# Fetching the first rounds' token rows of a mixture of experts from DRAM by index, instead of gathering them with one-hot products

## The reference

```python
hn = rmsnorm(h, norm_ffn_g[l])
# top-1 group of 4, then top-2 experts of its 8; combine holds the two weights of each token
for e in range(N_EXPERTS):
    h = jax.nn.silu(xf @ w_gate[e]) * (xf @ w_up[e])
    y = y + combine[:, e:e + 1] * (h @ w_down[e])
```

## Time and profile before

| | |
|---|---|
| median of 3 runs | 910.32 us (909.59 to 910.58) |
| the profiled execution | 909.68 us |
| its span, first to last instruction | 907.9 us |
| TensorE busy | 856.5 us, 94% |
| VectorE, ScalarE, GpSimd busy | 47%, 24%, 0% |
| moved by DMA | 246.86 MB, mean 272 GB/s |
| mean granted clock of TensorE | 0.98 |

### The profile page before, as it was taken

One profiled execution on the slowest core, in us unless ns is written; L12 is line 12 of the kernel. 1 busy time (PEld: TensorE's weight loads), 2 busy tenths in 40 slices (PEclk: granted clock), 3 DMA queues, 4 the chain that ended last, 5 costly groups with the idle time before them and its releaser, 6 DMA issues.

```text
span 907.9 us, 11349 instructions
## 1 busy us (share of the span) xinstructions
PE 856.5 (94%) x4631; PEld 553.3 (61%) x4631; DVE 426.2 (47%) x811; ACT 216.2 (24%) x397; POOL 3.7 (0%) x17
## 2 busy tenths in 40 slices
PE   8999999999999999999999985999996799999986
PEld 7888888777777888888734442453641353644532
DVE  5538325677674344436787122434332214435123
ACT  6422222464444222223211110100110001100114
POOL 0000000000000100000000000000000000000000
PEclk9999999999999999999999997999997899999998
DMA  8554212122222743692589999999999999999994
GB/s 291 143 98 115 97 47 93 47 93 69 72 93 66 222 115 93 266 403 75 204 320 428 417 427 427 427 427 427 429 426 430 428 427 427 427 430 426 426 412 188
DMA packets 68839, 246.86 MB, mean 272 GB/s; under 512 B 22536, under 2 KB 46128, under 8 KB 55216
## 3 DMA queue, kind: packets, MB, share of 16 engines
q1 hardware_dynamic: 68704, 246.07, 69.3%
q10 hardware_dynamic: 80, 0.02, 0.0%
HBM read 243.98 MB, written 2.10 MB: 271 GB/s over the span
## 4 chain that ended last, share of the span: by engine, by line
PE 83%; DMA 9%; DVE 4%; issue 2%; ACT 2%; SPq 0%; DVEq 0%; ACTq 0%
PE bank L904 18%; PE bank L591 9%; PE bank L593 9%; PE bank L592 9%; PE bank L961 8%; DMA R<-w_down 5%; DMA R<-w_up 3%; PE bank L618 2%; PE bank L619 2%; PE bank L620 2%; PE bank L870 2%; PE by_side L870 2%; PE bank L989 2%; PE bank L948 2%; PE bank L990 1%
## 5 line engine op out<-in xcount | busy, mean ns | idle before, releaser
L904 PE MATMUL bank<-R,packT 128*64 128x512 f32 (+1 forms) x1004 | 187.7, 611 | 20.1 <-DMA R<-w_up 10.6
L904 PEld LDWEIGHTS bank<-R,packT 128*64 128x64 f32 (+1 forms) x1004 | 58.7, 129 | 131.1 <-issue 130.6
L1438 DVE TENSOR_TENSOR wlo<-raw,whi 128x2048 fp32r<-128x2048 f32 x33 | 75.5, 2287 | 84.8 <-ACT whi L1139 84.7
L591 PE MATMUL bank<-xnT_hi,whi 128*128 128x512 f32 x288 | 113.6, 395 | 1.8 <-DVE wlo L1438 1.8
L593 PE MATMUL bank<-xnT_hi,wlo 128*128 128x512 f32 x288 | 112.2, 389 | 0.0
L592 PE MATMUL bank<-xnT_lo,whi 128*128 128x512 f32 x288 | 112.1, 389 | 0.0
L961 PE MATMUL bank<-R,actT 128*64 128x512 f32 (+1 forms) x384 | 73.8, 628 | 7.5 <-DMA R<-w_down 7.2
L1139 ACT ACTIVATE whi<-raw 128x2048 fp32r<-128x2048 f32 x33 | 63.0, 1908 | 67.7 <-PE by_side L593 33.8
L1920 DVE SCALAR_TENSOR_TENSOR y_lo<-bank,small,y_hi 128x512 fp32r<-128x512 f32 x26 | 19.4, 751 | 91.1 <-ACT y_hi L1338 91.1
L591 PEld LDWEIGHTS bank<-xnT_hi,whi 128*128 128x128 f32 x288 | 54.1, 188 | 13.3 <-issue 2.5
L593 PEld LDWEIGHTS bank<-xnT_hi,wlo 128*128 128x128 f32 x288 | 54.1, 188 | 11.5
(11 more groups left out here) (388 smaller groups left out, 1305.9 us busy)
## 6 DMA issues: line engine op xcount, KB each, us to landing
R<-w_up SPq DMA_DIRECT2D x28, 2048.0 KB, 18.4
R<-w_gate SPq DMA_DIRECT2D x26, 2048.0 KB, 19.7
R<-w_down SPq DMA_DIRECT2D x23, 2048.0 KB, 19.6
raw<-w_in SPq DMA_DIRECT2D x17, 1024.0 KB, 5.1
R<-w_down SPq DMA_DIRECT2D x10, 1024.0 KB, 10.0
R<-w_gate SPq DMA_DIRECT2D x8, 1024.0 KB, 9.9
R<-w_up SPq DMA_DIRECT2D x7, 1024.0 KB, 11.1
raw<-w_in SPq DMA_DIRECT2D x20, 256.0 KB, 4.5
```

The lines of the kernel that those rows point to most:

```text
L591: pe.matmul(dst, hi_w, hi_x, start=start, stop=False)
L904: mm = pe.matmul(dst[s * w:(s + 1) * w, :], packT[:, c, odd * P + s * w:odd * P + (s + 1) * w], part_of(s, c) if part_of else R[2 * slots[ ...
L1438: dve.tensor_tensor(wlo[c % 2][:, :], raw[c % 2][:, :], whi[c % 2][:, :].bitcast(F32), ALU.subtract).then_inc(lo_split, 1)
```

## The change

The normed rows are made whole in float32 (`hn`) and stored to a buffer in DRAM, `hn_rows`, one row per token behind a row of zeros for places that no token fills. For rounds 0, 1 and 2 TensorE no longer multiplies rows with masks. It multiplies the mask with the tokens' numbers (`number_rows`), which gives for each of the round's 128 rows the number of its token; VectorE writes it as an integer to `row_token`, and GpSimd issues an indirect DMA that fetches the 128 rows of 4 KB from DRAM into `rows` (`fetch_rows`). TensorE turns them (`turn_fetched`), ScalarE and VectorE copy them to `packT`. There is one buffer `rows`, so a fetch waits until the one before is turned. Masks are made 128 columns at a time (`mask_rows`), all first compares ahead of all second ones, instead of tile by tile.

`hn_hi` and `hn_lo` are made in round 2 (`high_h`, `low_h`), where round 3's rows are gathered with products as before, now behind the down products. `packT` is laid out by round first, and rounds 0 to 2 all use its first half. SyncE no longer waits for `hn_lo` ahead of L445; it waits for each tile of `hn` to store it, ahead of the wait for `logits_done`.

```diff
+    hn = at("hn", [P, TT, KT, P], F32, 96)
+    rows = at("rows", [P, KT * P], F32, 132)
+    hn_rows = nc.dram_tensor("hn_rows", [SEQ + 1, D], F32, kind="Internal").ap()
...
+            for t in range(TT):
+                sp.wait_ge(hn_ready, t + 1)
+                sp.dma_start(hn_rows[1 + t * P:1 + (t + 1) * P, :], hn[:, t, :, :].rearrange("p c q -> p (c q)")).then_inc(hn_stored, 16)
             sp.wait_ge(logits_done, TT)
             sp.dma_start(R[6][:, :], flat(w_gate, 2)).then_inc(slot_loaded[3], 16)
-            sp.wait_ge(hn_lo_ready, TT)
             sp.dma_start(first_down[1][:, :], flat(w_down, 0)[:, 4 * DE:8 * DE]).then_inc(spare_loaded, 16)
...
+            def fetch_rows(r):
+                if r:
+                    pool.wait_ge(left_turned, r)
+                    pool.wait_ge(right_turned, r)
+                pool.wait_ge(row_token_ready, r + 1)
+                pool.indirect_dma_start(out=rows[:, :], out_offset=None, in_=hn_rows[:, :],
+                                        in_offset=bass.IndirectOffsetOnAxis(ap=row_token[:, r:r + 1], axis=0)
+                                        ).then_inc(rows_landed, 16)
+            pool.wait_ge(hn_stored, 16 * (TT + 1))
+            for r in range(3):
+                fetch_rows(r)
...
+            def number_rows(r, b):
+                pe.wait_ge(masks_ready, TT * (r + 1))
+                for t in range(TT):
+                    mm = pe.matmul(bank[b][:, 0:1], onehot[:, t, r % 2 * P:(r % 2 + 1) * P].bitcast(F32), token_number[:, t:t + 1],
+                                   start=(t == 0), stop=(t == TT - 1))
+                mm.then_inc(tokens_summed, 1)
+            def turn_fetched(r, n, b):
+                pe.wait_ge(rows_landed, 16 * (r + 1))
+                for c in range(4 * n, 4 * n + 4):
+                    mm = pe.transpose(bank[b][:, c % 4 * P:(c % 4 + 1) * P], rows[:, c * P:(c + 1) * P], ident[:, :])
+                mm.then_inc((left_turned, right_turned)[n], 1)
...
-            keep_warm(1)
-            gather_first()
+            number_rows(0, 0)
+            keep_warm(2)
+            number_rows(1, 1)
+            keep_warm(2)
+            for n in range(2):
+                turn_fetched(0, n, 2 + n)
...
+                if i == 1:
+                    number_rows(2, 2)
...
+                elif i == 0:
+                    for n in range(2):
+                        turn_fetched(1, n, 2 + n)
...
+                if i == 1:
+                    pe.wait_ge(main.h_added, 2)
+                    turn_fetched(2, 0, 3)
+                    pe.wait_ge(main.actT_ready, 2)
+                    turn_fetched(2, 1, 4)
+                project_down(main, slots_of(i, 2), i, 8 * (i - 1) + 3 if i else None, None if i > 1 else down_half_done)
                 if i == 2:
                     pe.wait_ge(main.h_added, 8 * i)
+                    pe.wait_ge(main.onehot_ready, 1)
+                    pe.wait_ge(hn_lo_ready, TT)
                     for n in range(2):
-                        gather_half(1, n)
+                        gather_half(n)
                     for n in range(2):
-                        turn_gathered(1, n)
-                project_down(main, slots_of(i, 2), i, 8 * (i - 1) + 3 if i else None, None if i > 1 else down_half_done)
-                if i == 1:
-                    pe.wait_ge(main.h_added, 8 * i)
-                    pe.wait_ge(main.onehot_ready, 1)
-                    for n in range(2):
-                        gather_half(0, n)
-                    for n in range(2):
-                        turn_gathered(0, n)
+                        turn_gathered(n)
...
-                act.activation(hn_hi[:, t, :, :], hg[:, t, :, :], ACT.Copy, scale=rstd[:, t:t + 1]).then_inc(hn_hi_ready, 1)
+                act.activation(hn[:, t, :, :], hg[:, t, :, :], ACT.Copy, scale=rstd[:, t:t + 1]).then_inc(hn_ready, 1)
+            def high_h(t):
+                act.activation(hn_hi[:, t, :, :], hn[:, t, :, :], ACT.Copy).then_inc(hn_hi_ready, 1)
...
+            def mask_rows(r, numbers):
+                cols = slice(r % 2 * P, (r % 2 + 1) * P)
+                for t in range(TT):
+                    dve.tensor_scalar(onehot[:, t, cols], numbers[:, cols], row_first[:, t:t + 1], None,
+                                      ALU.is_equal).then_inc(mask_step, 1)
+                for t in range(TT):
+                    dve.wait_ge(mask_step, TT * r + t + 1)
+                    dve.scalar_tensor_tensor(out=onehot[:, t, cols], in0=numbers[:, cols], scalar=row_second[:, t:t + 1],
+                                             in1=onehot[:, t, cols].bitcast(F32), op0=ALU.is_equal,
+                                             op1=ALU.add).then_inc(masks_ready, 1)
...
+            pick_rows(ranks)
+            mask_rows(0, spaced_iota)
+            number_rows(0, 0)
+            mask_rows(1, spaced_iota)
+            number_rows(1, 1)
```

More of the change, by code:

```diff
@@ L331, in build_block, with packs_done @@
         PACK_BANKS = (2, 3, 7, 4)
+        def packs_done(line, g):
+            return 4 * g - 6 if line is main else 4 * g
         SPREAD_BANKS = ((2, 3, 5, 6), (7, 0, 1, 2))
@@ L883, in gather_half, with turn_gathered, project @@
                 mm.then_inc(main.pack_done, 1)
-            def turn_gathered(r, n):
-                pe.wait_ge((rows_left, rows_right)[n], r + 1)
+            def turn_gathered(n):
+                pe.wait_ge((rows_left, rows_right)[n], 1)
                 for c in range(4 * n, 4 * n + 4):
-                    mm = pe.transpose(bank[2 + n][:, c % 4 * P:(c % 4 + 1) * P], packT[:, c, r * P:(r + 1) * P], ident[:, :])
+                    mm = pe.transpose(bank[2 + n][:, c % 4 * P:(c % 4 + 1) * P], rows[:, c * P:(c + 1) * P], ident[:, :])
                 mm.then_inc((left_turned, right_turned)[n], 1)
-            def project(line, slots, odd, dst, done, packed=None, half_done=None, part_of=None, gathered=None):
+            def project(line, slots, side, dst, done, packed=None, half_done=None, part_of=None, gathered=None):
                 for slot, loaded in slots:
@@ L1011, in fill @@
                 pe.matmul(bank[b][:, 0:n], ident[:, :], h_tok[:, 0, 0:n], start=True, stop=True)
-            keep_warm(1)
-            gather_first()
+            number_rows(0, 0)
[4 more added lines that the diff above has]
+                turn_fetched(0, n, 2 + n)
             for i in range(LAST):
                 odd = i % 2
+                side = odd if i > 2 else 0
                 if i == OVER_AT:
@@ L1304, in copy_pack, with copy_rows @@
                                    ACT.Copy).then_inc(line.pack_a, 1)
[L1306 to L1312, removed]
+            def copy_rows(n):
+                act.wait_ge(main.pack_done, n + 1)
+                act.activation(rows[:, n * 512:(n + 1) * 512], bank[2 + n][:, :], ACT.Copy).then_inc((rows_left, rows_right)[n], 1)
@@ L1319, in expert_pair @@
                 act.wait_ge(line.gate_done, i + 1)
                 act.activation(silu_g[:, :], bank[0][:, :], ACT.Silu).then_inc(line.silu_ready, 1)
[L1321 to L1324, removed]
-                    for n in range(2):
-                        copy_turned(1, n)
-                    scale_rows(line, i, odd)
-                    return
+            def expert_pair(line, i, odd):
+                silu_rows(line, i)
@@ L1360, in _ @@
                         copy_pack(over, OV_PAIRS // 2)
-                expert_pair(main, i, i % 2, i == 2)
-                if i == 1:
-                    copy_rows(0, 0)
-                    copy_turned(0, 0)
-                elif i % 2:
-                    copy_pack(main, i // 2 + 1)
+                if i > 2:
+                    expert_pair(main, i, i % 2)
+                    if i % 2:
+                        copy_pack(main, i // 2 + 1)
+                    continue
+                silu_rows(main, i)
+                if i == 0:
+                    copy_turned(1, 0, 2)
+                if i == 2:
+                    act.wait_ge(main.up_done, 3)
+                    high_h(0)
+                    high_h(1)
+                copy_actT(main, i)
+                if i == 1:
+                    copy_turned(2, 0, 3)
+                if i == 2:
+                    high_h(2)
+                    high_h(3)
+                scale_rows(main, i, i % 2)
+                if i == 2:
+                    for n in range(2):
+                        copy_rows(n)
+                    for n in range(2):
+                        copy_turned(3, n, 2 + n)
             act.wait_ge(main.gate_done, LAST + 1)
@@ L1978, in _ @@
                     add_rows(main, i - 1)
+                if i == 1:
+                    copy_right(2, 4)
+                if i == 2:
+                    dve.wait_ge(hn_stored, 16 * (TT + 1))
+                    for t in range(TT):
+                        low_h(t)
                 low_y(main, i, i % 2)
-                if i == 1:
-                    copy_right_rows()
-                    copy_right_turned()
```

(2 more changed lines are left out.)

112 lines of the change are left out of this document (52 added, 60 removed).

## The result

| | before | changed |
|---|---|---|
| median of 6 runs | 910.45 us (909.27 to 911.28) | 918.18 us (916.46 to 920.55) |
| ratio | | 1.0089, 95% interval 1.0071 to 1.0108 |
| the profiled execution, its span | 909.68 us, 907.9 us | 920.16 us, 918.4 us |
| TensorE busy | 856.5 us | 858.9 us |
| moved by DMA | 246.86 MB | 250.52 MB |

The prediction said 911.2 us with a range to 917.0. The loss is 7.7 us by the medians, 10.5 us by the two profiled spans, which I take apart first.

The account below looks back on a forecast made before the run. From 460 us a fixed number of bytes at the DMA rate bounds the kernel. Start -0.3 and bytes +1.2 give +0.9 us on the profiled 909.68, so 910.6; the median lies 0.64 higher: 911.2 us, range 908.5 to 917.

Parts of the forecast that it names:

- Everything else is hidden: Rounds 1 to 3: moving round 3's gather behind round 2's down products costs nothing, its 5 to 6 us covered by weights.
- The later high and low parts: Round 2: four on ScalarE at 1.1 and four on VectorE at 1.3 us are hidden; uncovered, about 5 us.
- The start: Round 0: gate products start at 453.6 us after masks, number products, fetch and transposes, 0.3 us earlier than before.
- The bound: From 460 us on, the span is a fixed number of bytes at the DMA rate plus a short tail.
- fetch 2's bytes: Round 2's fetch, read inside the full weight stream: 0.52 MB at 427 GB/s adds 1.2 us.
- stores at no cost: Before round 0: storing the normed rows, four times 512 KB, lands by 444 us, ahead of the fetch, and costs nothing.
- TensorE's 5 us less in round 1: Round 1's half gather, about 5 us, leaves TensorE; listed among the hidden work, so no gain counted.
- The late fetch: Rival, round 0: slow descriptors or reads make the first fetch late, 913.9 to 916.8 us; chance 0.20.
- VectorE didn't hold GpSimd up: Rival, first fetch: VectorE's second masks hold GpSimd back, landing 1.7 us later, +2.6 us, 912.9 us; chance 0.08.
- Clock at half through the gate products: Rival, round 0: half clock lasts through the gate products though the fetch is in time, 914.1 us; chance 0.13.
- Early: Rival, round 0: quick masks and fetch at full clock start gate products at 451.3, total 908.9 us; chance 0.11.
- TensorE as the bound: Rival, whole kernel: TensorE is the limit, so round 1's 5 us of removed gather count, about 906 us; chance 0.06.

Follow-up runs that it names:

- run 10: The kernel before without the branch on the number of overflow tiles ahead of round 3, overflow rounds left out: 909.48 us, ratio 0.9997.
- run 2: The kernel before with only round 3's product gather moved behind round 2's down products, ScalarE's copies along with it: 913.21 us, ratio 1.0039.
- run 6: The changed kernel with high and low parts made in round 1 and round 3's gather ahead of round 2's down products: 913.66 us, ratio 1.0051.
- changed_again: Run 5: the changed kernel measured once more with no edit: 917.62 us, ratio 1.0088.
- 9: The changed kernel without the branch on the number of overflow tiles ahead of round 3, overflow rounds left out: 913.27 us, ratio 1.0045.
- run 1: The changed kernel with round 3's gather put back ahead of round 2's down products, ScalarE's copies along with it: 920.67 us, ratio 1.0122.
- run 11: The kernel of run 6 with one more pair of fillers ahead of the first number products: 913.1 us, ratio 1.0042.
- run 4: The kernel before with five more fillers ahead of the first gather, to start round 0 late: 912.72 us, ratio 1.0033.
- run 8: The kernel of run 6 without the fetch for round 2, whose experts work on round 1's rows: 912.34 us, ratio 1.003.

## Why the prediction was wrong

**The step that failed: "Everything else is hidden ... the next gate products wait for weights until 558.44 anyway."** They didn't. Between the down products of round 2 and 558.44 there lie the halves of y, spread, eight adds of 4.9 us and 6.4 us of branch, and no weights (run 10: without the branch 552.18). The row at 558.44 had no DMA ahead of it in the chain, only "issue" behind the adds to h_tok; I had taken idle TensorE beside full queues for a wait on them. So the gather behind the down products lengthened a serial path. It has slack, 5.7 - 3.6 = 2.1 us by run 2, and what exceeds the slack dries the stream. In the changed kernel this can be worked out: the weights came 5.9 us later (543.53 against 537.62), the gate products 12.8 us; the 6.9 us between them less 2.1 of slack leave 4.8, where the windows lose 4.4 and, with the one at 670 us, 5.3. Worth by runs: 3.6 us (2), 4.0 (6 against 5), 4.1 (9 against 5: 3.8 us above its own kernel before, against 7.9). Without this part the time would have been near 914 us, inside the range.

**A second part of that step: TensorE without the gather idles, and loses its clock.** In the changed kernel the down products of round 2, behind 6 us of waiting, take 9.82 us instead of 7.11. In the kernel before the gather stood in that wait, ahead of the products, and they ran at full clock; in run 6 it stands there again, and they take 7.05 us. It made the path longer by another 2.7 us. "The later high and low parts ... lie in round 2, where both wait" cost the changed kernel nothing that a run shows, but run 1 shows their price: they are ready 5 us too late for the gather to go back to its gap.

**The start, "0.3 us earlier than now": wrong in sign.** Measured +4.34 in the profiled execution and +2.1 in the second; by runs 9 and 6, where the stream is whole, start and bytes together are 3.8 and 4.0 us of time. With bytes at 1.2 that leaves 2.6 to 2.8 for the start, yet in the profiled executions of these two kernels the gate products start only 1.5 us late (455.33 and 455.37); the rest, about 1 us, no run explains. By its terms:

| term | predicted | measured |
|---|---|---|
| VectorE has the ranks | 443.01 | 443.59 |
| masks | 1.7 us | 1.9 us |
| number products | 0.6 us | 1.69 (1.05 in `changed_again`) |
| copy, then way to GpSimd | 0.2 us | 0.16 + 0.85 us |
| GpSimd starts | 446.5 | 449.22 |
| issue to landing | 5.3 us | 4.5 us |
| a pair of fillers | 1.8 us | 3.62, at full clock 1.8 |
| transposes | 451.8 to 453.2 | 456.92; 453.33 in run 11, at full clock, as the rows land |

The fetch itself was well bounded, even a little cheaper than I took it. What cost was ahead of it (2.7 us) and the half clock beside it. I had weighed half clock until 451.3 as the worst; it lasted until 457. The Trainium skill's page "DMA: Bandwidth & Descriptors" (Anatomy of one DMA) would give 3.2 us, an estimate from that page; the trace doesn't agree, 4.5 us at an idle time and 9.5 us in the full stream of weights.

**Right.** The bound (a stream of fixed bytes from 460 us on) and with it one to one from start to end (run 4); fetch 2's bytes, 1.2 us (run 8: 1.3, within noise); stores at no cost (SyncE's next transfer went out at 437.59, in the kernel before at 437.10, and GpSimd's wait ended on VectorE's copy, not on them). That TensorE's 5 us less in round 1 are worth nothing by themselves fits the wait for w_down behind them, but no run takes out only that. Fetch 2 was issued at 492.23, not 485.04: 4.4 us of this are the late start, and the rest are `turn_weights`, the number products, which follow the gate products, and the way to GpSimd. It landed at 501.7, ahead of its transposes at 502.21, so TensorE didn't wait for it; round 1's down products came 1.8 us later than the shift alone makes them (503.08 against 496.99, less 4.34) because of the number products (0.79 us) and the transposes (0.87 us), and the gather's absence took that up.

**The rivals.** The late fetch (913.9 to 916.8 us) had the right sign, and the start was as late as it said and more, but its cause, descriptors or slow reads, was not the one: the waits and products ahead of the fetch were, and the half clock. VectorE didn't hold GpSimd up by its second set of masks: they ran until 450.2, the indirect DMA started at 449.22, and it landed 4.5 us later, like fetch 1 (4.6), which has no masks beside it. The 1.7 us by which such a lock, of which the Trainium skill's page "SBUF — State Buffer" (SBUF: two separate sides) warns, was to delay the fetch are not seen here. A hold of a few tenths can't be excluded, since VectorE was at work beside all three fetches. Clock at half through the gate products: no, 7.09 us; it fell on the fillers ahead and on round 2's products. Early: no, GpSimd started 2.7 us later than forecast. TensorE as the bound: no, the time rose.

**What stays open.** What part of the 7.7 us in the medians is start and what is its variation is known only to about 1 us, since a profile shows one execution. What makes the 0.8 us from VectorE's copy to GpSimd's start was not tried; behind TensorE's transposes, ahead of fetch 1, it was 0.75 us, so it doesn't hang on the copy.

## What to carry to other kernels

An idle engine beside full DMA queues isn't proof that it waits for data: follow the chain into the idle time, and if it goes through "issue" and other engines, it is a serial path whose slack must be measured before work is moved onto it. In a stream-bound kernel ask which product frees the next slot, and keep its delay relative to the weights below that slack. And work that stands in a wait has a second use: taken out, it leaves an engine idle, and here the next products then started at half clock.

## What the runs showed of the hardware

- The branch on a loaded number takes TensorE 6.1 to 7.1 us after its last wait, in every run that has it.
- An indirect DMA of 128 rows of 4 KB: 0.94 to 1.16 us on GpSimd, 0.8 us from its last wait to its start, 4.3 to 4.8 us from issue to landing when the queues are idle or nearly so, 8.7 to 9.5 us in the full stream (profiled executions of all kernels with a fetch).
- A float32 product with one moving column isn't cheap: four of them (eight instructions) took 0.79 us at full clock and up to 1.88 us with the clock at half; four 128x128 transposes (four instructions) took 0.45 us at full clock.
- Behind 2.9 us of waiting the granted clock stood at 1.00 when the number products began and at 0.50 in 447:448, while they ran; it stayed there through fillers and number products until 457 us. In another execution of the same program it fell in 449:450, under the fillers, and the second pair of fillers, from 452.96, was at full clock again.
